# Gram products of two heads issued in alternation into four PSUM banks, in a one-core RWKV-7 and attention block

## The reference

```python
cols = rms_norm(h, norm_pre_mix) @ w_in            # q,k,v | RWKV r,k,v and LoRA parts | two gates
o_attn = banded_gqa_attention(q, k, v, sink)
o_rwkv = rwkv7_bidirectional(...)                  # 32 heads of 64, a forward and a backward scan, summed
# per direction, per head, step by step:
sa = S @ a_t
S  = S * w_t + sa b_t^T + v_t k_t^T
y  = S @ r_t
...
y = (group_norm(y_f + y_b) + bonus) * g            # g = sigmoid(gd) @ g_up
mix = (sigmoid(g_attn) * o_attn + sigmoid(g_rwkv) * o_rwkv) @ w_out
h = h + rms_norm(mix);  h = h + rms_norm(relu(rms_norm(h) @ w_ffn_up)**2 @ w_ffn_down)
```

## Time and profile before

| | |
|---|---|
| time, median of 3 runs | 2393.41 us (2392.64 to 2393.51) |
| span of the profiled execution | 2389.9 us |
| PE busy | 2237.5 us (94%) |
| PEld busy | 2035.3 us (85%) |
| DVE busy | 1343.1 us (56%) |
| ACT busy | 909.8 us (38%) |
| POOL busy | 449.7 us (19%) |

### The profile page before, as it was taken

How to read it: one execution, slowest core, us unless ns; L and a number is a source line. 1 busy time by engine, 2 the same in 40 slices (tenths; PEclk the granted TensorE clock), 3 DMA queues, 4 the chain that set the end, 5 groups by cost and what they waited for, 6 DMA issues and landing times.

```text
span 2389.9 us, 40964 instructions
## 1 busy us (share of the span) xinstructions
PE 2237.5 (94%) x15563; PEld 2035.3 (85%) x15563; DVE 1343.1 (56%) x2119; ACT 909.8 (38%) x1384; POOL 449.7 (19%) x424
## 2 busy tenths in 40 slices
PE   6999997999999999999999987979999999999996
PEld 6999996899988888899988876769889789798894
DVE  4666465666656666666666652355555455454454
ACT  4554432343433333333433322344334333343342
POOL 0000001444434443344444431000000000000000
PEclk9999997999999999999999965989999999999998
DMA  7556662222222221222222210544656556556552
GB/s 204 141 138 162 172 167 71 72 64 76 74 60 69 65 76 53 76 58 76 74 60 58 76 36 6 188 141 148 177 179 184 168 183 176 177 180 173 180 185 89
DMA packets 415086, 281.27 MB, mean 118 GB/s; under 512 B 14042, under 2 KB 372668, under 8 KB 414012
## 3 DMA queue, kind: packets, MB, share of 16 engines
q1 hardware_dynamic: 414620, 277.43, 40.1%
q10 hardware_dynamic: 416, 3.15, 0.3%
HBM read 278.46 MB, written 2.10 MB: 117 GB/s over the span
## 4 chain that ended last, share of the span: by engine, by line
issue 51%; PE 35%; DVE 6%; POOL 5%; ACT 2%; DMA 0%; SPq 0%; POOLq 0%; DVEq 0%; ACTq 0%
PE bank L1343 6%; PE bank L1344 5%; PE bank L1345 5%; PE bank L1599 3%; PE bank L1620 3%; PE bank L1617 3%; PE bank L1359 1%; PE bank L1360 1%; PE bank L1361 1%; POOL st L1271 1%; DVE wlo L741 1%; PE bank L1549 1%; POOL AR L1281 1%; PE bank L1415 1%; DVE Pd L969 1%
## 5 line engine op out<-in xcount | busy, mean ns | idle before, releaser
L1343 PE MATMUL bank<-xT,whi 128*128 128x256 f32 x2784 | 824.3, 296 | 13.1 <-PE bank L1361 5.2
L741 DVE TENSOR_TENSOR wlo<-raw,whi 128x2048 fp32r<-128x2048 f32 (+1 forms) x286 | 549.3, 1921 | 491.8 <-ACT whi L405 431.3
L1344 PE MATMUL bank<-xT,whi 128*128 128x256 f32 x2784 | 787.3, 283 | 0.0
L1345 PE MATMUL bank<-xT,wlo 128*128 128x256 f32 x2784 | 786.9, 283 | 0.0
L1343 PEld LDWEIGHTS bank<-xT,whi 128*128 128x128 f32 x2784 | 533.4, 192 | 23.1 <-issue 18.5
L1344 PEld LDWEIGHTS bank<-xT,whi 128*128 128x128 f32 x2784 | 533.8, 192 | 1.2
L1345 PEld LDWEIGHTS bank<-xT,wlo 128*128 128x128 f32 x2784 | 532.3, 191 | 0.0
L405 ACT ACTIVATE whi<-raw 128x2048 fp32r<-128x2048 f32 x166 | 316.9, 1909 | 288.1 <-PE bank L1361 288.1
L1359 PE MATMUL bank<-whi,ft 128*128 128x512 f32 x512 | 205.4, 401 | 12.2 <-PE bank L1361 9.2
L1303 POOL TENSOR_TENSOR CT<-G,lmk 128x512 fp32r<-128x512 f32 x160 | 185.0, 1163 | 114.8 <-PE bank L1599 114.7
L1360 PE MATMUL bank<-wlo,ft 128*128 128x512 f32 x512 | 202.2, 395 | 0.0
(11 more groups left out here) (214 smaller groups left out, 3194.3 us busy)
## 6 DMA issues: line engine op xcount, KB each, us to landing
raw<-in_w_in SPq DMA_DIRECT2D x106, 1024.0 KB, 5.9
raw<-in_w_ffn_up SPq DMA_DIRECT2D x64, 1024.0 KB, 6.4
raw<-in_w_ffn_down SPq DMA_DIRECT2D x64, 1024.0 KB, 5.0
raw<-in_w_out SPq DMA_DIRECT2D x16, 1024.0 KB, 5.0
raw<-in_w_in SPq DMA_DIRECT2D x4, 768.0 KB, 4.5
xtok<-in_x SPq DMA_DIRECT2D x2, 1024.0 KB, 5.9
upg<-in_g_up SPq DMA_DIRECT2D x16, 128.0 KB, 3.4
hres<-in_x ACTq DMA_DIRECT2D x1, 2048.0 KB, 10.7
```

The costliest lines, as they stand in the source:

```text
L741: x = V.tensor_tensor(wlo[:, u_static % 2, part], raw[:, u_static % 4, part], whi[:, u_static % 2, part].bitcast(f32), ALU.subtract)
L1343: M(bank[:, 0:T], h, xT[:, k, 0, :], start=k == 0, stop=False)
L1344: M(bank[:, 0:T], h, xT[:, k, 1, :], start=False, stop=False)
L1345: x = M(bank[:, 0:T], l, xT[:, k, 0, :], start=False, stop=k == KT - 1)
```

## The change

The eight Gram products become four calls `heads(g)`, g = 2d + tb. Each issues four instructions: `ta` of head 0, `ta` of head 1, `kh` of head 0, `kh` of head 1, and increments `gram` once, at the last. heads(0) and heads(2) write banks 3 and 2, heads(1) and heads(3) banks 5 and 4. `keep(m)` waits for call m // 2 and reads the bank to match; DVE's order is left as it is. In the tail, no Gram product stands between the gate product and mean any more; heads(0) follows mean, heads(1) follows var, heads(2) and heads(3) follow vbc. The gate product moves to the second half of bank 6, and ACT's copy of it waits for `bonv` besides. The first transposes move from bank 5 to bank 3 and wait for keep(5); the second stay in bank 6 and wait for `gups`, ACT's copy of the gate product.

```diff
-                    self.w("gram", m + 1)
+                    bank = PB[(3 if m // 2 % 2 == 0 else 5) - m % 2]
+                    self.w("gram", m // 2 + 1)
...
                 def gate(self):
-                    pe.wait_ge(s["rese"].sem, s["rese"].before(self.n))
+                    pe.wait_ge(s["sme"].sem, s["sme"].before(self.n))
...
-                def gram(self, m):
+                def heads(self, g):
...
-                    if m >= 2:
-                        w("gmask", m - 1)
-                    elif m == 0:
+                    if g >= 2:
+                        w("gmask", 2 * g - 2)
+                    elif g == 0:
                         w("tas")
-                    else:
                         w("tws")
                         pe.wait_ge(s["ye"].sem, s["ye"].before(self.n))
-                    hp, ts = slice(64 * h, 64 * h + 64), slice(P * tb, P * tb + P)
+                    else:
+                        w("vts")
+                        pe.wait_ge(s["rese"].sem, s["rese"].before(self.n))
+                    ts = slice(P * tb, P * tb + P)
                     for a, src in enumerate((bh[d], kh[d])):
-                        x = M(PB[3 - q % 2][:, T * a:T * a + T], src[hp, ts], AR[d][hp, :, ts], start=True, stop=True)
+                        for h in range(2):
+                            hp, bank = slice(64 * h, 64 * h + 64), PB[(3 if g % 2 == 0 else 5) - h]
+                            x = M(bank[:, T * a:T * a + T], src[hp, ts], AR[d][hp, :, ts], start=True, stop=True)
                     inc(x, "gram")
...
                     if d == 0:
                         w("vts")
+                        w("gmask", 6)
                     else:
                         w("bonv")
+                        w("gups")
...
                 if gram:
                     gram.gate()
-                    gram.gram(0)
                     nx.w("nkk")
                 w("ye")
                 x = M(PB[7][:, 0:T], ones_mean, ysb[:], start=True, stop=True)
                 inc(x, "mean")
                 if gram:
-                    gram.gram(1)
-                    gram.gram(2)
+                    gram.heads(0)
                 w("ysqs")
...
                 if gram:
-                    gram.gram(3)
-                    gram.gram(4)
+                    gram.heads(1)
                     gram.bonus()
                 w("vrep")
...
                 if gram:
-                    for m in range(5, 8):
-                        gram.gram(m)
+                    gram.heads(2)
+                    gram.heads(3)
```

More of the change, by code:

```diff
@@ L242, in block_kernel @@
             kAB=1, rkd=1, lw=1, la=1, lg=1, tws=1, decs=2, tas=1, gups=1, scan=2, inv=2, ar=2, tt=2, bhs=2, km1=2, km2=2,
-            khs=2, kbs=1, t2=1, vtp=1, vts=1, gram=8, gmask=8, dt0=2, d0p=2, d0=2, ctm=12, wmm=12, wev=12,
+            khs=2, kbs=1, t2=1, vtp=1, vts=1, gram=4, gmask=8, dt0=2, d0p=2, d0=2, ctm=12, wmm=12, wev=12,
             ddm=10, dtm=12, dup=10, dtup=12, kbtp=1, kbs2=1, rhsm=2, rhsc=2, um=2, ue=2, resm=2, rese=2, dum=2, due=2,
@@ L602, in pair @@
                 w("lg")
-                A.activation(gup[:], PB[4][:, 0:T], ACT.Copy).then_inc(s["gups"].sem, 1)
+                w("bonv")
+                A.activation(gup[:], PB[6][:, T:2 * T], ACT.Copy).then_inc(s["gups"].sem, 1)
                 A.activation(gt[:], raw4[:, 3, 1:T + 1], ACT.Tanh, scale=0.5).then_inc(s["gate_t"].sem, 1)
@@ L606, in pair @@
                     w("d0p", d + 1)
-                    A.activation(Dm[d][:].rearrange("p a b -> p (a b)"), PB[5 + d][:, :], ACT.Copy).then_inc(s["d0"].sem, 1)
+                    A.activation(Dm[d][:].rearrange("p a b -> p (a b)"), PB[3 + 3 * d][:, :], ACT.Copy).then_inc(s["d0"].sem, 1)
                     cut_pair(1, d1, d)
@@ L1019, in keep @@
                     inc(V.copy_predicated(G[d][:, q, :, :].rearrange("p (a b) c -> p a (b c)", a=2), mask,
-                                          PB[3 - q % 2][:, :].rearrange("p (a b) -> p a b", a=2)), "gmask")
+                                          bank[:, :].rearrange("p (a b) -> p a b", a=2)), "gmask")
                 def lasts(self):
@@ L1524, in gate @@
                 def gate(self):
-                    pe.wait_ge(s["rese"].sem, s["rese"].before(self.n))
+                    pe.wait_ge(s["sme"].sem, s["sme"].before(self.n))
                     for q in range(2):
-                        x = M(PB[4][:, 0:T], upg[:, q, :], gact[:, q, :], start=q == 0, stop=q == 1)
+                        x = M(PB[6][:, T:2 * T], upg[:, q, :], gact[:, q, :], start=q == 0, stop=q == 1)
                     inc(x, "lg")
-                def gram(self, m):
+                def heads(self, g):
                     w = self.w
-                    d, q = m // 4, m % 4
-                    tb, h = q // 2, q % 2
-                    if q == 0:
+                    d, tb = g // 2, g % 2
+                    if tb == 0:
                         w("khs", d + 1)
@@ L1578, in pair @@
                         w("vts")
+                        w("gmask", 6)
                     else:
                         w("bonv")
+                        w("gups")
                     for q in range(4):
-                        x = nc.tensor.transpose(PB[5 + d][:, P * q:P * q + P], DT[d][:, q, :].bitcast(f32), ident)
+                        x = nc.tensor.transpose(PB[3 + 3 * d][:, P * q:P * q + P], DT[d][:, q, :].bitcast(f32), ident)
                     inc(x, "d0p")
@@ L1592, in blocks_w @@
                         if d == 0:
-                            w("gups")
                             w("gmask", 8)
@@ L1761, in _ @@
             g0.gate()
-            for m in range(8):
-                g0.gram(m)
-                if m == 3:
+            for g in range(4):
+                g0.heads(g)
+                if g == 1:
                     g0.bonus()
```

## The result

| | changed kernel | kernel before, in the same rounds |
|---|---|---|
| time, median of 4 runs | 2413.26 us (2411.32 to 2416.86) | 2393.02 us (2392.44 to 2393.51) |
| ratio, 95% interval | 1.0086 (1.0072 to 1.01) | |
| span of the profiled execution | 2412.4 us | 2389.9 us |

What follows compares the result with a forecast made beforehand. DVE's last masked copy was taken to bound PE in each tail. A longer chain of 21.6 us, less 3.0 ahead of the loop, plus 18.3 for the clock, made 37 us: 2430 us forecast, range 2406 to 2460.

Steps and rivals of the forecast that it cites:

- What bounds the kernel: Tail of the pair loop: DVE's last masked copy, through POOL's DT, sets when PE passes the second transposes.
- Rival C: Tail: PE's stream decides, not DVE's chain; 51 us less, 2342 us; chance 0.07.
- The chain: Tail: masked copies and second transposes 1.4 us later in 14 tails, 2.0 in the last; 21.6 us in all.
- keep(0) 0.71 later: Tail: DVE's first masked copy waits for heads(0) behind mean and starts 0.71 us later than before.
- heads(1) behind var: Tail: the costly move; heads(1) is issued only after var, so keep(2) starts 1.47 us later.
- Rival D: Heads calls: alternating heads do not overlap, a call costs 2.1 us; about 2453 us; chance 0.08.
- my 1.20: Assumed time from the start of a heads call until its results are there, 1.20 us, bounds 1.08 and 1.39.
- Ahead of the loop: Gram products before the pair loop: four banks let calls go back to back, gaining 3 us, bounds 1 and 3.6.
- The clock: Pair loop: more falls to 1.2 GHz from PE's empty time, 8.3 plus 10 us, 18.3 in all; bounds 0 and 37.
- The falls in the tail: PE's empty time before var and vbc: falls in about 12 of 15 tails, 8 more, at 1.04 us each; 8.3 us.
- the falls behind the second transposes: Inversion levels after the over 2 us wait: falls in half of the pairs at 1.4 us, up to 1.7; 10 us.
- Rival B: Pair loop: the chain lengthens but the clock falls no more often than before; 2412 us; chance 0.20.

Runs made afterwards that it cites:

- centre first: Changed kernel with DVE doing centre ahead of keep(0) instead of behind it; 2449.13 us, ratio 1.0226.
- experiment 4: Changed kernel with unread products on PE, three ahead of var and four ahead of the second transposes; 2396.73 us, ratio 1.0014.
- experiment 8: Changed kernel, but ahead of the loop each heads call waits for both masked copies of the call before, as with one bank set; 2421.03 us.
- experiment 3: Changed kernel with three unread products on PE between heads(0) and the wait of var; 2427.22 us, ratio 1.0112.
- split early: Changed kernel with centre before keep(0), four unread products before second transposes, DVE's half weight split before centre, heads(2) before vbc; 2363.62 us, ratio 0.987.
- experiment 2: Changed kernel with DVE's centre exchanged with keep(0), so that centre goes first; 2449.13 us, ratio 1.0226.
- experiment 7: Changed kernel with heads(1) issued right behind heads(0), ahead of var; 2477.59 us, ratio 1.0354.
- experiment 10's control: Changed kernel with centre before keep(0), half weight split before centre, heads(2) before vbc, but without the four unread products; 2421.04 us, ratio 1.0111.
- the best version: Changed kernel with centre before keep(0), four unread products before second transposes, half weight split before centre, heads(2) before vbc; 2363.62 us, ratio 0.987.

## Why the prediction was right, and where its sizes were off

**What bounds the kernel: right.** DVE's last masked copy still sets when PE goes on. In the changed kernel 0.67 us more at keep(7) are 0.64 more at the second transposes, and 0.6 to 0.7 more in the pair; in "centre first" 0.77 less at keep(7) are 0.8 less in the pair. Rival C (PE's shorter stream decides) is out: dense filler starts 9.64 after the gate product instead of 10.87, 1.23 earlier, and all of it, with the 0.64 us by which the transposes are late, went into the wait, 2.05 us instead of 0.18.

**The chain: right in kind, too big in size.** It was to cost 21.6 us, 1.4 in a tail and 2.0 in the last. Measured it is 0.63 in a tail and 2.5 in the last, which has a fall of the clock in it. From the first gate product to the last pair's second transposes, the kernel before takes 953.3 us with 4 falls at 1.1 to 1.3, so some 948.8 without; experiment 4, with the chain and without falls in 13 pairs, takes 960.5. That is 11.7 us: 13 times 0.63, 1.0 and 2.5. Of the 2.5 an estimated 1.5 are the fall, since keep(4) starts 10.36 us after the gate product there and 8.90 in the tails without one. So the chain by itself is nearer to 10 us, less than half of the forecast. The term mis-sized was **keep(0) 0.71 later**. It was 0.45: the gate product's slot took 0.97, where I had given mean the time at which a product of 64 rows started, 1.06 behind the gate product; mean to heads(0) took 0.52 instead of 0.63; and the call's results were there 1.14 us after its start instead of 1.20. That the first slot is shorter because mean has the gate product's form of 128 rows is likely but wasn't tested. The second step, **heads(1) behind var**, was the costly one as said, but keep(2) came 0.98 later and not 1.47: 0.26 of the difference is that of keep(0), the rest shorter steps up to the square and from var to heads(1), 0.54. By keep(4) it was 0.86, and keep(7) made up 0.19 more, which no step of mine had; it lies in add_bonus, 0.44 us long here and 0.63 in the kernel before (see the last section).

Rival D (alternating heads don't overlap) is out: a call takes 1.14 us, and one head after the other does it in the same. The Trainium skill, "TensorE: Matmul & The Clock Gate", Part 3, would have four instructions of two row groups cost hardly more than those of one; the earlier trace rows had 1.06 for the slot of one product that stands alone, and here two cost a slot of 1.06 (heads(1) from 533.22 to the bonus product at 534.28). By that rule, the trace agrees, and my 1.20 was too dear by 0.06, not the 0.1 that the rule had.

**Ahead of the loop: right in kind, too small in size.** 3.0 us were forecast, at most 3.6. The first gate product came 4.8 us earlier, and counted from the first Gram product 6.6 (74.0 against 80.65). I had counted at half clock throughout. With the second set of banks the clock rose on the way, which experiment 8 shows by taking that set away.

**The clock: right in its sum, half right in its places.** 18.3 us were forecast. Experiment 4 against the changed kernel gives 979.8 - 960.5 = 19.3 us of falls in the loop; less some 4.5 of the kernel before, 14.8 are the change's, or some 16 with the fall in the last tail that experiment 4 has too. The falls in the tail were forecast in 12 of 15 at 1.04 each, and came in 13 at 1.0 (68.4 against 67.4), but four of them 6.8 us long. Of the falls behind the second transposes, forecast in half of the pairs, there were two. The mechanism was real, though: where the first falls were filled away they came in 12 pairs at 0.9 each and once for 44 us (experiment 3), and where the chain was shortened they came at 19.6 to 22.8 us each. My bound of 1.7 us for such a fall was far too low, as it took for granted that it would last 3.4 us.

**The sum.** 11.7 + 14.8 - 4.8 = 21.7 us, against 22.5 in the span; the other 0.8 us came behind the loop. Of the 22.5, the 1.9 by which the changed kernel's trace was late at its Gram products (experiment 8) came ahead of all that the change touches, so 20.6 would be the change's, near the 20.2 between the medians. I had also put the median 3.5 us above the span, and it lay 0.9 above. Rival B, the chain without more falls, had named 2412, very near the time that came, by luck. It had the chain nearly twice too dear and left out the falls: with the measured chain it would have named some 2400 us (2393.0 + 11.7 - 4.8, an estimate), and the falls are two thirds of the loss or more. The Trainium skill, "TensorE: Matmul & The Clock Gate", section "HAM oscillation", makes a fall the price of idle gaps between bursts. What spoke against it was how short the gaps are here; yet gaps of 1.6 and 2.05 us were followed by falls, and filling both took the falls away. So the runs agree with the page on the cause and not on the length: the gaps here are much shorter than the waits of its example.

## What to carry to other kernels

When an edit takes work from an engine that later waits, ask first what it delays on the engine that is waited for, and in which slot the first result that it needs now comes out; the saved time is only empty time moved. And read the clock in every empty place that an edit makes on PE, before and behind it: here two waits of 1.6 and 2 us cost more than the longer chain, an improvement of 1.5 us a pair turned into a loss of 2.3%, and four unread products in the wait turned that into a gain of 0.9%. Where nobody waits, such products cost their full time, 1.7 us in pair 0. A fixed chain with empty places on two engines is worth reordering by what each step waits for (centre first, split early), but only with the clock held.

## What the runs showed of the hardware

**How long a fall lasts depends on where it begins.** Falls behind the first empty place lasted 3.4 us and cost 1.0, or 6.8 us and cost 1.5 to 1.8 (pairs of 68.83 and 69.20 us in experiment 8). Behind the second transposes two kinds stand close together. In the first 14 pairs of all traces of kernels that left the filler in its place, all 24 falls that began between 0.1 us before and 0.8 us after the start of the second transposes lasted 3.4 us. All 17 that began 1.07 to 1.57 us after it lasted 44.4 to 54.6 us: ten in experiment 2, three in experiment 7, one in experiment 3, three in experiment 10's control. Two pairs of experiment 7, first one with a short fall, then the one with the long stretch that is shown there:

```profile
901.65 0.88 PE L1588 MATMUL bank<-cst,DT 128*128 128x128 f32 x4 [2.06 <-POOL DT L1298]
...
902.00:905.40 3.40, 3.40 (x18) 3.40 (x17) 1.23 (x1) 2.14 (x3) 1.47 (x2) 0.51 0.00 0
...
811.98 0.66 PE L1588 MATMUL bank<-cst,DT 128*128 128x128 f32 x4 [2.04 <-POOL DT L1298]
...
813.18 0.93 PE L1604 MATMUL bank<-Dm,CT 128*128 128x128 f32 x4
```

The first fall begins on the dense filler that follows the transposes, the second (at 813.2) where the small products of the inversion levels (L1604) begin. PE's records cover the long stretch wholly (51.20 of 51.20 us), so no empty place inside it explains its length, and the clock comes back before the pair ends. What keeps it down in the levels, and why the same gap is followed by a fall in one pair and by none in its neighbour, no run settles.

**DVE and POOL hold one another up.** An addition on DVE of two operands in SBUF (add_bonus, L1066) that starts while POOL's `CT` runs ends 0.28 us after `CT`, however early it started; where it starts later, as in the four tails of the kernel before that have a fall, it takes 0.41 us. In the changed kernel POOL's `CT` ends at 539.39:

```profile
538.22 1.17 POOL L1300 TENSOR_TENSOR CT<-G,lmk 128x512 fp32r<-128x512 f32 x1
```

and add_bonus at 539.23 + 0.44 = 539.67. In the best version `CT` ends at 535.97 and the addition at 536.25:

```profile
534.79 1.18 POOL L1300 TENSOR_TENSOR CT<-G,lmk 128x512 fp32r<-128x512 f32 x1
```

```profile
535.27 0.98 DVE L1066 TENSOR_TENSOR yc<-yc,bon 128x256 f32<-128x256 f32 x1 [0.18 <-ACT yc L654]
```

In the kernel before, add_bonus ends at 877.92, again 0.28 us behind `CT`, at 877.64:

```profile
876.49 1.15 POOL L1299 TENSOR_TENSOR CT<-G,lmk 128x512 fp32r<-128x512 f32 x1
```

```profile
877.29 0.63 DVE L1065 TENSOR_TENSOR yc<-yc,bon 128x256 f32<-128x256 f32 x1
```

In the best version this is where 0.54 of the 1.34 us went that it had won at keep(4). In the other direction, POOL's first `DT` took 1.95 us in the changed kernel and 1.16 in the best version:

```profile
536.31 1.95 POOL L1298 TENSOR_TENSOR DT<-G,lmk 128x512 fp32r<-128x512 f32 x1 [1.73 <-DVE G L1020]
```

```profile
533.68 1.16 POOL L1298 TENSOR_TENSOR DT<-G,lmk 128x512 fp32r<-128x512 f32 x1 [1.21 <-DVE G L1020]
```

In the changed kernel it began while DVE's split, also with two operands in SBUF, ran to 537.24, and ended 1.02 us behind it; in the best version the split isn't there any more. The Trainium skill, "GPSIMD Engine Reference", section "1. Specifications", says that POOL's SBUF interfaces are shared with VectorE and that DVE's instructions of two SBUF inputs contend for them; the traces agree, and show it as one waiting for the other's end. No run here took the two apart by themselves.
